# A two-layer recurrent decoder trunk: the norms between its stages in two sides of 160 tokens

## What is computed

```
x += 0.5 * post1(SwiGLU1(pre1(x)))
x += postm(Mix(prem(x)))
x += 0.5 * post2(SwiGLU2(pre2(x)))
rmsnorm(x, g) = x * rsqrt(mean(x*x) + 1e-6) * g
swiglu(x) = (silu(x @ wg) * (x @ wu)) @ wd          # inner width 2816
```

## Time and profile before

| | |
|---|---|
| median of 3 runs | 2145.59 us (2145.29 to 2145.84) |
| the profiled execution's own time | 2146.02 us |
| its span, first to last instruction | 2143.9 us |
| PE busy | 98% of the span |
| PE's weight loads | 86% |
| DVE, ACT busy | 62%, 38% |
| granted TensorE clock, mean | 1.00 of full |
| DMA | 118 GB/s on the mean |

### The profile page before, as it was taken

The page is one execution under the profiler, slowest core; times in us unless marked ns, Lnnn a source line. Parts: engine busy times, 40 slices in busy tenths (PEclk is TensorE's granted clock), DMA queues, the critical chain, the costliest instruction groups (busy, mean ns, idle before and its releaser), DMA issues.

```text
span 2143.9 us, 30994 instructions
## 1 busy us (share of the span) xinstructions
PE 2092.4 (98%) x12624; PEld 1844.9 (86%) x12624; DVE 1322.6 (62%) x1987; ACT 817.9 (38%) x932; POOL 39.3 (2%) x74
## 2 busy tenths in 40 slices
PE   7999999999999999999999999999999999999998
PEld 6999997777766699999999999977777667999998
DVE  4564586776556676555376645766765576765644
ACT  5554451112143145554355534412121422455542
POOL 1000000000000000000000000000000000000000
PEclk9999999999999999999999999999999999999999
DMA  5434431111133243444434443211111323434442
GB/s 210 152 143 157 156 118 38 58 51 70 45 110 120 91 158 118 157 148 147 170 138 146 155 157 138 105 40 52 68 51 65 121 90 130 163 113 149 145 156 103
DMA packets 38067, 252.13 MB, mean 118 GB/s; under 512 B 4720, under 2 KB 4912, under 8 KB 9424
## 3 DMA queue, kind: packets, MB, share of 16 engines
q1 hardware_dynamic: 33120, 234.60, 30.7%
q0 software_dynamic: 4848, 16.13, 2.0%
HBM read 242.05 MB, written 8.67 MB: 117 GB/s over the span
## 4 chain that ended last, share of the span: by engine, by line
PE 85%; DVE 8%; ACT 3%; DVEq 2%; issue 1%; DMA 0%; SPq 0%; ACTq 0%
PE dps L600 42%; PE dps L539 15%; PE dps L489 11%; DVE tmp L1252 2%; PE mx L698 2%; PE mx L692 2%; PE mx L700 2%; ACT tmp L922 1%; PE mx L556 1%; PE mx L809 1%; DVEq L1717 1%; PE mx L845 1%; DVE tmp L1468 1%; DVE rs L1310 1%; DVE tmp L1598 1%
## 5 line engine op out<-in xcount | busy, mean ns | idle before, releaser
L539 PE MATMUL dps<-u,raw 128*128 128x320 f32 x1536 | 478.3, 439 | 0.0
L600 PE MATMUL dps<-uh,whi 128*128 128x320 f32 x1408 | 430.0, 305 | 16.2 <-DVE wlo L1249 15.8
L1249 DVE TENSOR_TENSOR wlo<-raw,whi 128x2048 fp32r<-128x2048 f32 x136 | 311.7, 2292 | 214.7 <-ACT whi L922 209.6
L600 PE MATMUL dps<-uh,wlo 128*128 128x320 f32 x1408 | 434.3, 308 | 0.0
L600 PE MATMUL dps<-ul,whi 128*128 128x320 f32 x1408 | 432.9, 307 | 0.0
L922 ACT ACTIVATE whi<-raw 128x2048 fp32r<-128x2048 f32 x138 | 262.9, 1905 | 380.2 <-PE dps L600 370.0
L539 PEld LDWEIGHTS dps<-u,raw 128*128 128x128 f32 x1536 | 269.5, 190 | 89.2 <-issue 13.7
L600 PEld LDWEIGHTS dps<-uh,whi 128*128 128x128 f32 x1408 | 264.8, 188 | 20.9 <-issue 16.9
L600 PEld LDWEIGHTS dps<-uh,wlo 128*128 128x128 f32 x1408 | 264.9, 188 | 0.0
L600 PEld LDWEIGHTS dps<-ul,whi 128*128 128x128 f32 x1408 | 263.9, 187 | 0.6
L600 PE MATMUL dps<-hfh,whi 128*128 128x320 f32 x704 | 220.4, 313 | 0.0
(11 more groups left out here) (302 smaller groups left out, 3022.1 us busy)
## 6 DMA issues: line engine op xcount, KB each, us to landing
raw<-in_wstream SPq DMA_DIRECT2D x220, 1024.0 KB, 4.8
hs<-in_st_hgrn POOLq DMA_DIRECT2D x8, 512.0 KB, 6.2
out_o_hgrn<-hs POOLq DMA_DIRECT2D x8, 512.0 KB, 2.9
sw<-in_smallw POOLq DMA_DIRECT2D x2, 1024.0 KB, 6.8
ss<-in_st_rwkv POOLq DMA_DIRECT2D x8, 256.0 KB, 3.9
out_o_rwkv<-ss POOLq DMA_DIRECT2D x8, 256.0 KB, 2.3
x<-in_xT SPq DMA_DIRECT2D x4, 320.0 KB, 4.5
out_yT<-x SPq DMA_DIRECT2D x4, 320.0 KB, 2.2
```

What stands on the lines that cost most here:

```text
L539: m = pe.matmul(dps[:, 2 * s + c, 0:T], w[:, k, c * P:(c + 1) * P], u[:, k, :], start=k == 0, stop=k == KD - 1, skip_group_check=True)
L600: m = pe.matmul(dps[:, 2 * half + c, 0:T], w[:, k, c * P:(c + 1) * P], v[:, k0 + k, :], start=first and k == 0 and i == 0, stop=last and k ...
L1249: return nc.vector.tensor_tensor(out, a, b, op)
```

## The change

The tokens are cut in two sides, t = 0 for columns 0 to 159 and t = 1 for 160 to 319, wherever a norm between stages is near.
- At an end (the last group of an FFN, the last two half blocks of w_out) PE does all products of side 0, then all of side 1, each of 160 columns with its own weight load. Side 0 goes to banks of `dps`, side 1 to banks of `mx` (`last_tiles`). After 12 products of side 1's last block PE closes side 0's sum of squares; side 1's comes at the end behind one call of `keep_busy`.
- ACT and DVE do the post norm and the renewal of x side by side in time: root, reciprocal and pairs for side 0, then for side 1.
- At an entry, behind three calls of `keep_busy`, PE does side 0 of both blocks (of half blocks 0 to 3 in the mixer), then side 1. The splits of the second block's or the halves' weights take other places in ACT's and DVE's lists.
- The output goes in eight stores instead of four.
- In the last HGRN2 head five dense pieces go behind the norm's sum.

The diff, cut to what matters:

```diff
--- before.py
+++ after.py
...
+SIDES = (slice(0, T // 2), slice(T // 2, T))
...
+
+        def last_tiles(t):
+
+            return (dps[:, 2:4, :], mx[:, 0:2, :])[t][:, :, SIDES[t]]
...
-                sp.dma_start(yT[:, 2 * j:2 * j + 2, :], x[:, 2 * j:2 * j + 2, :]).then_inc(S["y_stored"], 16)
-            sp.wait_ge(S["y_stored"], 64)
+            for t, side in enumerate(SIDES):
+                for j in range(4):
+                    sp.wait_ge(x_new[t], 3 * L * 4 + j + 1)
+                    sp.dma_start(yT[:, 2 * j:2 * j + 2, side], x[:, 2 * j:2 * j + 2, side]).then_inc(S["y_stored"], 16)
+            sp.wait_ge(S["y_stored"], 128)
 
 
         @block.gpsimd
...
+            def mixer_entry(l):
...
+                for s in range(2):
+                    pair_wait(l, Q_A // 2, s)
+                keep_busy(dps[:, 0, :], 3)
+                for t, side in enumerate(SIDES):
+                    for j in range(4):
+                        u_wait(l, 1, t, j)
+                        for h in range(H_A):
+                            for k in (2 * j, 2 * j + 1):
+                                m = product(mx[:, h, side], h, k, 0, (uh, ul), k == 0, k == KD - 1, side)
+                            if t == 1 and j == 3:
+                                m.then_inc(S["half_done"], 1)
+                        pre_sum(l, 1, t, j)
+                    for h in range(H_A, H_A + 2):
+                        if t == 0:
+                            pe.wait_ge(S["half_lo"], l * NHALF + (h + 1))
+                        for k in range(KD):
+                            m = product(dps[:, h - H_A, side], h, k, 0, (uh, ul), k == 0, k == KD - 1, side)
+                        if t == 1:
                             m.then_inc(S["half_done"], 1)
...
+            def added_sum(l, i, t):
+
+                pe.wait_ge(S["sq_added"], l * 3 + (i + 1))
+                pe.matmul(mx[:, 3 - t, SIDES[t]], ones, sq[:, 0, SIDES[t]], start=True, stop=False, skip_group_check=True)
+
+            def last_sum(l, i, t):
+
+                pe.wait_ge(sq_last[t], l * 3 + (i + 1))
+                for k in (6, 7):
+                    m = pe.matmul(mx[:, 3 - t, SIDES[t]], ones, sq[:, k, SIDES[t]], start=False, stop=k == 7,
+                                  skip_group_check=True)
+                m.then_inc(post_done[t], 1)
+
+            def closing_sum(l, i):
+
+                keep_busy(mx[:, 2, :], 1)
+                added_sum(l, i, 1)
+                last_sum(l, i, 1)
+
...
             def ffn(l, b, q, f):
...
-                for s in range(2):
-                    split_in(0, s)
-                    pair_wait(l, q // 2, s)
-                    split_tiles(s, KD, uh[:, :, :], ul[:, :, :], s, norm=None if s else (l, 2 * f))
+                for t, side in enumerate(SIDES):
+                    for s in range(2):
+                        if t == 0:
+                            split_in(0, s)
+                            pair_wait(l, q // 2, s)
+                            if s == 0:
+                                keep_busy(dps[:, 0, :], 3)
+                        for j in range(4):
+                            if s == 0:
+                                u_wait(l, 2 * f, t, j)
+                            for c in range(2):
+                                for k in (2 * j, 2 * j + 1):
+                                    m = split_product(s, KD, uh, ul, s, c, k, True, True, 0, side)
+                            if t == 1 and j == 3:
+                                m.then_inc(S["block_done"], 1)
+                            if s == 0:
+                                pre_sum(l, 2 * f, t, j)
...
-                post_sum(l, 4 * f + 1)
+                    kt = 8 if part < 2 else 6
+                    if half < 3:
+                        split_tiles(j % 2, kt, hfh, hfl, half % 2, first=part == 0, last=part == 2, k0=8 * part)
+                        continue
+                    for t, side in enumerate(SIDES):
+                        for c in range(2):
+                            for k in range(kt):
+                                if j == 11 and (t, c, k) == (1, 0, 4):
+                                    added_sum(l, 2 * f, 0)
+                                    last_sum(l, 2 * f, 0)
+                                m = split_product(j % 2, kt, hfh, hfl, 1, c, k, part == 0, part == 2, 8 * part, side,
+                                                  last_tiles(t)[:, c, :])
+                        if t:
+                            m.then_inc(S["block_done"], 1)
+                        elif j == 11:
+                            m.then_inc(S["first_done"], 1)
+                closing_sum(l, 2 * f)
...
                 pe.matmul(mx[:, 2, 0:P], kt3[:, 0, :], vt3[:, 0, :], start=True, stop=True)
                 pe.matmul(mx[:, 2, P:2 * P], kt3[:, 1, :], vt3[:, 1, :], start=True, stop=True)\
                     .then_inc(S["hst1_done"], 1)
-                dense_part(1)
+                if p < 3:
+                    dense_part(1)
...
 
                 def low_rank(kind):
 
...
-                two_halves(l, 2)
                 two_halves(l, 4)
                 low_rank(0)
...
-                post_sum(l, 3)
+                pe.wait_ge(S["half_lo"], l * NHALF + NHALF)
+                pair_wait(l, (Q_OUT + 3) // 2, 1)
+                for t, side in enumerate(SIDES):
+                    for c in range(2):
+                        for k in range(KD):
+                            if (t, c, k) == (1, 0, 4):
+                                added_sum(l, 1, 0)
+                                last_sum(l, 1, 0)
+                            m = product(last_tiles(t)[:, c, :], NHALF - 2 + c, k, 0, (merged_hi, merged_lo),
+                                        k == 0, k == KD - 1, side)
+                        if t == 1:
+                            m.then_inc(S["half_done"], 1)
+                    if t == 0:
+                        m.then_inc(S["first_done"], 1)
+                closing_sum(l, 1)
...
+
+            def root(l, i, t):
+
+                act.wait_ge(post_done[t], l * 3 + (i + 1))
+                fn(rt[:, SIDES[t]], mx[:, 3 - t, SIDES[t]], ACT.Sqrt, scale=1.0 / D, bias=epst[:, 0:1])\
+                    .then_inc(post_root[t], 1)
...
+            def enter(l, n, name, t, j):
+
+                act.wait_ge(x_new[t], l * 12 + (4 * n + j + 1))
+                for k in (2 * j, 2 * j + 1):
+                    m = fn(uh[:, k, SIDES[t]], x[:, k, SIDES[t]], ACT.Copy, scale=gain(l, name, k))
+                m.then_inc(uh_ready[t], 1)
+                square(t, j)
...
+            def read_last(l, t, name):
+
+                side = SIDES[t]
+                fn(sq[:, 6:8, side], last_tiles(t), ACT.Square).then_inc(sq_last[t], 1)
+                for c in range(2):
+                    m = fn(ho[:, 6 + c, side], last_tiles(t)[:, c, :], ACT.Copy, scale=gain(l, name, 6 + c))
+                if t == 1:
                     m.then_inc(pair_free[1], 1)
...
-                act.wait_ge(S["first_done"], l * 2 + f + 1)
+                act.wait_ge(S["first_done"], l * 3 + (2 * f + 1))
                 read_last(l, 0, post)
+                root(l, 2 * f, 0)
                 wait_block(act, l, f, KF + 11)
                 read_last(l, 1, post)
-                root(l, 4 * f + 1)
                 if f == 0:
+                    following = l, 1, "mix_pre_g"
+                    enter(*following, 0, 0)
+                    enter(*following, 0, 1)
+                    root(l, 0, 1)
                     high(l, 2)
+                    enter(*following, 0, 2)
+                    enter(*following, 0, 3)
+                    high(l, 3)
                 elif l < L - 1:
+                    following = l + 1, 0, "ffn1_pre_g"
+                    enter(*following, 0, 0)
+                    enter(*following, 0, 1)
+                    root(l, 2, 1)
+                    enter(*following, 0, 2)
+                    enter(*following, 0, 3)
                     split_hi(l + 1, 0, 1, 1, 0)
-                if next_norm(l, f):
-                    enter(*next_norm(l, f))
-                    if f == 0:
-                        high(l, 3)
-                    root(next_norm(l, f)[0], 2 * next_norm(l, f)[1])
+                else:
+                    root(l, 2, 1)
+                    return
+                for j in range(4):
+                    enter(*following, 1, j)
+                pre_root(*following[:2])
...
-                for c in range(2):
-                    wait_half(act, l, NHALF - 2 + c)
-                    read_last(l, c, "mix_post_g")
-                root(l, 3)
                 split_hi(l, 0, 1, 1, 1)
-                enter(l, 2, "ffn2_pre_g")
-                root(l, 4)
+                act.wait_ge(S["first_done"], l * 3 + 2)
+                read_last(l, 0, "mix_post_g")
+                root(l, 1, 0)
+                wait_half(act, l, NHALF - 1)
+                read_last(l, 1, "mix_post_g")
+                for t in range(2):
```

(110 more changed lines are left out.)

182 lines of the change are left out of this document (54 added, 128 removed).

## The result

The kernel after takes **2255.76 us** (median of 4 runs, 2253.33 to 2257.05) against 2145.45 (4 runs, 2145.29 to 2145.84): ratio 1.0513, 95% interval 1.0494 to 1.0531. Forecast: 2216.5, range 2138 to 2250. The direction is right; 39 us are missing, and the measurement lies just above the range.

The account below looks back on a forecast made before the run. PE's own stream was taken to bound the kernel (busy 98%). Terms of +88.8, -25.0, +6.3, +4.4, +1.5, -3.0 and -2.1 sum to +70.9 us on 2146.0; less 0.4 to the median, 2216.5 us, range 2138 to 2250.

Parts of the forecast that it names:

- Price of a side product: At entries and ends, 1200 products become 2400 of 160 columns at 0.110 us each instead of 0.146: +88.8 us.
- (a): Rival: the floor is full fp32's alone, a one-pass side product costs 0.080 us; 2158 us, chance 10%.
- (b): Rival: a side product costs only its bare stream, 0.067 us, so faster than before; 2140 us, chance 8%.
- (c): Rival: a side product costs 0.146 us, as much as a whole one; 2295 us, chance 3%.
- (d): Rival: a short product goes in four passes like fp32, 0.268 us each; 2585 us, chance 9%.
- The gap: At five borders, last to first useful PE product takes 2.8 us instead of 7.84: -5.0 each, -25.0 us.
- First entry: Three dummy calls before the first product, at the lower clock level, take 2.6 us and displace later products: +1.5 us.
- Inside the entries: PE waits inside entries: 3.6 at FFN to mixer, 2.1 at the layers' border, 0.2 per FFN entry: +6.3 us.
- Behind the FFN entries: PE waits for the next weight split because the last 48 products are shorter: +1.1 at each of four, +4.4 us.
- Tail: From the last product to the end of the stores takes 10.9 us instead of 13.9: -3.0 us.
- Last head: Five dense pieces moved behind the last norm's sum cover a wait of 1.06 us: -2.1 us for two layers.

Follow-up runs that it names:

- experiment 5: Kernel before, with only the last-group products of the four FFN ends issued as two of 160 columns, same order; 2185.85 us, ratio 1.0182.
- 8: Kernel after with whole products in the first entry and four dummy calls in the layers' border wait, without the three first dummies; 2204.26 us.
- 3: Kernel after with whole 320-column products in the first FFN entry and four more dummy calls in the wait at the layers' border; 2207.43 us.
- experiment 9: Kernel after, all sides kept, with dummies: eighteen before the first FFN (replacing three), five ending the first entry, four at the layers' border; 2211.97 us.
- 12: Kernel before with eighteen dummy calls ahead of its first feed-forward part; 2144.13 us against 2146.55, ratio 0.999.
- experiment 2: Kernel after with four more dummy calls in PE's wait at the border of the layers; 2219.0 us.
- 10: Kernel after with eighteen dummy calls ahead of the first feed-forward part in place of the first entry's three; 2232.78 us.
- 11: Kernel after with seven dummy calls instead of three ahead of its first side product; 2234.7 us.
- Experiment 6: Kernel before with only the five dense pieces of the last HGRN2 head moved behind its norm's sum; 2145.6 us, ratio 0.9997.
- 1: Kernel after with the first FFN entry's products whole again over 320 columns, its three dummies kept; 2223.29 us.
- experiment 4: Kernel before with each first-FFN-entry product issued as two of 160 columns, sums whole, no dummies ahead; 2155.77 us, ratio 1.0045.
- 7: Kernel before with four dummy calls instead of 15 at each post norm; 2155.11 us, ratio 1.0035.

## Why the prediction was wrong, point by point

- **Price of a side product, +88.8: right.** 0.111 against 0.110; in experiment 5 the 528 cuts of the FFN ends cost 1.82% (1.66 to 1.97), +39 us (36 to 42), where the same price gives +40.9. Rivals (a) to (d) fall. The bare stream of 0.067 (0.133 for 320 columns) in (a) and (b) is an estimate from the 2.4 above; the runs show 0.111 and 0.146, and neither stream bare. The sums' fp32 instructions of 160 columns go at 0.135 (299.17 to 299.82 is four and one product), those of 320 at 0.268 (845.14 to 846.36 before), as forecast.
- **The gap, -25.0: right.** 2.6 us where 2.8 was forecast.
- **First entry, +1.5: the step that failed.** It priced three dummies at the lower level (2.6 us; from 15.17 to the second product at 18.00, less one of 0.213, they take 2.6) and took for granted, without a reason, that the clock rises as early as before. The dummies cost 0.9 (8 against 3), but the clock rose at 69.15 and not by 19.73, and all side products up to there went at 0.213. Post-norm reciprocal of the first FFN: 293.13 in the kernel after, 268.38 with the clock held (experiment 9): **24.7 us**. The sum held 3.6 of these: 1.5 for the dummies, and 2.1 for the low start that the kernel before has too (12). About 21 are missing from it.
- **Inside the entries, +6.3: failed as well; waits right, their consequence put at nothing.** The 2.1 us at the border of the layers are there (1.6 of PE, 1.9 of its loads), but were priced as a wait alone. The clock fell after them and side products kept it low. From the reciprocal before this border (1139.66) to the next post norm's (1404.82) is 265.16; in experiment 9, 1114.79 to 1363.24 is 248.45: **16.7 us**. The mixer's entry takes 26.7 (297.74 to 324.46), forecast 26.
- **Behind the FFN entries, +4.4: right where the clock is up.** In the kernel after only the second FFNs wait, 0.93 each; the first entry and that of layer 1 were at the low level and had no such wait. With the clock held three wait 0.93, and the first entry waits 2.46 (experiments 2, 10 and 11; in 9 dummies fill it) where it waited 0.84 before: 2.8 + 1.6 = 4.4.
- **Tail, -3.0: right.** From the last product's end (2240.93) to the span's end (2251.6) is 10.7, against 10.9 forecast.
- **Last head, -2.1: not shown.** Experiment 6: no change in the time that can be told; 0.67 less in the layer where the clock stayed up.

The whole: one period, from the first post norm's reciprocal of layer 0 to that of layer 1, takes 1060.46 before and 1094.85 in experiment 9: +34.4. The prediction's terms for it are 3 ends (9.8 + 9.8 + 3.6), 3 entries (21.3), three gaps (-15.0), waits of 4.3 and 2.2, and one head (-1.06): +34.9. In span, after less before is 107.7. With the clock held it is 66.2 (2210.1 less 2143.9); the forecast without its first dummies (1.5) and with the first products at the upper level (2.1) is 70.9 - 3.6 = 67.3. The other 41.5 are the two stretches (24.7 + 16.7 = 41.4), of which the sum held 3.6. A part of the closeness is luck: experiment 9 has a short fall of some 3 us at 672, for which no term stands. The sum of +70.9 was that of a kernel whose clock stays as it was; the range had no case for one that does not: its bounds came from the price of a side product, the gap and the waits alone.

**What is shown and what isn't.** Shown: undoing either low stretch, by whole products or by dummies, gives its time back (1, 9, 10, 11). At the layers' border the four builds that leave the wait of 1.6 us empty (the kernel after, 1, 10, 11) all fall there, and the four with dummies in it (2, 3, 8, 9) do not: 263.6 to 265.2 us between the two reciprocals against 248.4. In 5 and in the trace of 10 the side stream did not itself make the clock fall. Open is when exactly a wait makes it fall: one of 2.5 us for the next low part, behind the first entry's products, was followed by a low stretch of nearly 7 us in experiment 2, by one half as long in 11, and by none in 10. Why the same first entry rose at once in experiment 2 and not in the kernel after is open as well; PE's start differed by 0.65 us, and with more dummies a still later start rose. Why the cut entry of experiment 4 came up after 8 us is open too.

## What to carry to other kernels

Before cutting matmuls into shorter ones, look where PE starts or waits: a wait of 1.6 us ahead of a stream of short products cost 17 us here, while ahead of whole products five emptied borders cost 8 us together (7). Put dummies into that wait, or let whole products follow it (as in 7), and warm TensorE up in the time in which it waits for its first weights (2255.76 to 2232.78 in 10). And when a change makes PE's instructions shorter, give the clock a term of its own in the sum, with a bound from rows at the low level (here 0.213 against 0.111 for each product of an entry).

## What was not expected of the hardware

- A busy PE did not bring the clock back: in the kernel after it worked without a gap on side products from 17.5 to 67.3 and from 1144.2 to 1178.1 (with sums of 160 columns among them), 0.213 apart. The clock rose 1.9 and 3.6 us after the first whole product; elsewhere it rose in whole products (19.50 in 1), in or just behind a whole fp32 sum (by 19.73 before), among side products just behind such a sum (22.67 in 4), or in or just behind dummies (17.6 in 2, by 20.46 in 11).
- Short falls of about 3 to 7 us turn up inside the mixers, at other places in each build (696 after, 768 in experiment 2, 756 in 3, 660 in 4, 744 in 6, 672 in 9, 768 and 1791 in 11; none before, nor in 1, 5, 7, 8, 10 and 12). In that of the kernel after six fp32 instructions of 320 columns go at 0.53 (696.92 to 700.11), 16 behind it at 0.27 (700.85 to 705.15): it costs about half its length. What sets such falls off was not tried.
